# Taking unread matrix products out of the routing stage of a two-layer mixture-of-experts encoder

## The reference

```python
def expert_choice_moe(x, w_router, b_router, w_gate, w_up, w_down):
    cap = EC_CAPACITY_FACTOR * s // N_EXPERTS            # 2*512/16 = 64 tokens for each of 16 experts
    logits = (x @ w_router) + b_router                   # 512 tokens x 16 experts
    aff = jax.nn.softmax(logits, axis=-1)
    gates, idx = lax.top_k(aff.transpose(0, 2, 1), cap)  # each expert picks its 64 tokens
    xs = x[idx]
    hid = silu(xs @ w_gate[e]) * (xs @ w_up[e])          # 64x1024 @ 1024x1024, per expert
    o = (hid @ w_down[e]) * gates
    y = zeros.at[idx].add(o)                             # back to the tokens

for l in range(2):
    mix = concat(attention, short conv, conformer conv, windowed attention) @ w_out[l]
    x = layer_norm(alpha * x + mix)
    x = layer_norm(alpha * x + expert_choice_moe(x))
```

## Time and profile before

| | us |
|---|---|
| median of 3 runs | 1485.55 |
| profiled execution | 1484.97 |
| its span | 1483.0 |
| PE busy | 1368.4 (92%) |
| DVE busy | 495.6 (33%) |
| routing and expert stage, first layer | about 258 to 732 |
| routing and expert stage, second layer | about 989 to 1465 |

### The profile page before, as it was taken

One profiled execution on the slowest core, in us unless ns is written; L12 is line 12 of the kernel. 1 busy time (PEld: TensorE's weight loads), 2 busy tenths in 40 slices (PEclk: granted clock), 3 DMA queues, 4 the chain that ended last, 5 costly groups with the idle time before them and its releaser, 6 DMA issues.

```text
span 1483.0 us, 15565 instructions
## 1 busy us (share of the span) xinstructions
PE 1368.4 (92%) x6362; PEld 714.1 (48%) x6362; DVE 495.6 (33%) x999; ACT 292.5 (20%) x517; POOL 107.6 (7%) x90
## 2 busy tenths in 40 slices
PE   6999999999999999989789998999999999999884
PEld 5666668533343333333367565774343343343332
DVE  5774754410211111101449557451201201201205
ACT  2336540110000000000033456211000000000000
POOL 1330000000000000000133200000000000000001
PEclk9999999999999999999979999999999999999998
DMA  9300351999999999999960012539999999999994
GB/s 384 116 1 1 142 199 49 417 421 429 427 426 427 427 426 427 427 427 428 421 242 1 0 55 89 214 143 428 428 428 426 428 426 429 426 426 429 426 428 168
DMA packets 43685, 462.03 MB, mean 312 GB/s; under 512 B 7776, under 2 KB 8416, under 8 KB 14944
## 3 DMA queue, kind: packets, MB, share of 16 engines
q1 hardware_dynamic: 33120, 436.88, 69.8%
q0 software_dynamic: 3744, 13.63, 2.3%
q10 hardware_dynamic: 6752, 10.54, 2.1%
HBM read 450.55 MB, written 10.49 MB: 311 GB/s over the span
## 4 chain that ended last, share of the span: by engine, by line
PE 75%; DMA 12%; DVE 6%; issue 3%; ACT 3%; SPq 0%; ACTq 0%; DVEq 0%; POOLq 0%
PE bank L896 24%; PE bank L919 13%; PE bank L520 10%; DMA ring<-w_moe 10%; PE bank L864 8%; PE bank L775 2%; PE bank L779 2%; PE bank L778 2%; PE bank L757 2%; PE bank L478 2%; PE bank L835 1%; PE bank L664 1%; PE bank L941 1%; PE bank L748 1%; PE bank L852 1%
## 5 line engine op out<-in xcount | busy, mean ns | idle before, releaser
L896 PE MATMUL bank<-ring,work 128*64 128x512 f32 x1600 | 350.4, 593 | 16.2 <-issue 8.8
L896 PEld LDWEIGHTS bank<-ring,work 128*64 128x64 f32 x1600 | 131.0, 137 | 221.7 <-issue 195.7
L919 PE MATMUL bank<-ring,w_up 128*64 128x512 f32 x832 | 187.3, 600 | 16.2 <-ACT w_up L1787 10.9
L1474 DVE TENSOR_TENSOR work<-work,bank 128x512 f32<-128x512 f32 x32 | 22.0, 687 | 476.9 <-PE bank L896 476.1
L1493 DVE TENSOR_TENSOR X<-X,bank 128x512 f32<-128x512 f32 x112 | 77.0, 688 | 251.4 <-PE bank L864 251.4
L919 PEld LDWEIGHTS bank<-ring,w_up 128*64 128x64 f32 x832 | 65.2, 138 | 127.4 <-issue 109.9
L864 PE MATMUL bank<-work,cst 128*128 128x512 f32 x240 | 116.3, 617 | 9.8 <-ACT work L1808 9.8
L896 PE MATMUL bank<-work 128*64 128x512 f32 x448 | 99.0, 593 | 1.5 <-issue 1.5
L520 PE MATMUL bank<-x_hi,w_hi 128*128 128x512 f32 x288 | 82.6, 434 | 11.1 <-ACT x_hi L1561 6.2
L864 PEld LDWEIGHTS bank<-work,cst 128*128 128x128 f32 x240 | 38.5, 188 | 87.2 <-DVE X L1493 36.7
L1132 DVE SCALAR_TENSOR_TENSOR bank<-X,par,bank 128x512 f32<-128x512 f32 x120 | 79.9, 749 | 0.9 <-DVE ring L1106 0.9
(11 more groups left out here) (223 smaller groups left out, 1531.6 us busy)
## 6 DMA issues: line engine op xcount, KB each, us to landing
ring<-w_moe SPq DMA_DIRECT2D x154, 2048.0 KB, 27.4
work<-w_moe SPq DMA_DIRECT2D x36, 2048.0 KB, 22.7
ring<-w_in SPq DMA_DIRECT2D x18, 1024.0 KB, 19.9
ring<-w_out SPq DMA_DIRECT2D x8, 1024.0 KB, 32.0
out<-X POOLq DMA_DIRECT2D x12, 512.0 KB, 10.3
X<-out ACTq DMA_DIRECT2D x2, 2048.0 KB, 8.2
work<-ln SPq DMA_DIRECT2D x4, 1024.0 KB, 18.5
x_rows<-X ACTq DMA_DIRECT2D x8, 512.0 KB, 2.7
```

The lines of the kernel that those rows point to most:

```text
L896: ins = mm(B((kind, pair, n))[64 * e:64 * e + 64, :], xsT[:, k, 64 * e:64 * e + 64], w[:, e, n * 512:(n + 1) * 512], start=(k == 0), stop= ...
L919: ins = mm(B(("O", pair, n))[64 * e:64 * e + 64, :], hidT[:, k, 64 * e:64 * e + 64], w[:, i, e], start=(k == 0), stop=(k == KD - 1))
```

## The change

The function `unread` and its three calls are gone; no other instruction is added, removed or moved.

```diff
-                def unread(times):
-
-                    for i in range(times):
-                        mm(B(("O", 0, 1))[:, :], ident, cos_d[:], start=True, stop=True)
-
...
                 pe.sem_inc(freed, 1)
 
 
-                unread(1)
                 pe.wait_ge(tokens_in, at(lay, 16, 16))
                 pe.wait_ge(aff_ready, at(lay, 1, 1))
                 before(pe, ("affT",), lay)
...
                 ins.then_inc(fullsem(("affT",)), 1)
-                unread(8)
 
 
                 pe.wait_ge(edge_ready, at(lay, 1, 1))
...
                     .then_inc(fullsem(("rank",)), 1)
-                unread(1)
```

## The result

The changed kernel takes 1489.31 us (median of 9 runs, 1487.27 to 1490.42) against 1484.5 us (9 runs, 1482.56 to 1486.66) of the kernel before: ratio 1.0029, 95% interval 1.002 to 1.0039. It is 4.8 us or 0.29% slower, above the 0.2% under which the prediction would have called it no change. The time lies in the forecast range, in its upper third; the likeliest case had been +1.6 us and "no change". Its profiled execution took 1489.66 us, with a span of 1487.7 us.

The account below looks back on a forecast made before the run. The weight queue was taken to set each layer's end; PE 2.5 and 3.3 us late, less slack of 1.8 and 2.4, gave pauses of 0.7 and 0.9 us: 1484.97 + 1.6 = 1486.6 us, range 1484.0 to 1491.5.

Parts of the forecast that it names:

- the likeliest case: Whole kernel: a pause of up to 4.5 us in the weight queue, +1.6 us taken; chance 0.52.
- What bounds the kernel: From the logits on, the weight queue sets each layer's end; a late PE costs only if the queue runs empty.
- The hold-up of L811: Routing: the eight middle unread products hold up the edge product; removal gains 0.76 us in the first layer, nothing in the second.
- The chain at half clock: L811 to L823 in the routing: eleven small records at 0.12 us more each, 1.3 us per layer, between 0 and 1.4.
- The dense run after it: The gather from L835 starts at half clock for 4.0 us and loses 2.0 us per layer, between 1.4 and 2.65.
- rival B: The gather does not bring the clock back; all its records run cold, pauses together 9.2 us, 1494.2 us; chance 0.12.
- PE's lateness: After the routing PE is later than now by 2.5 us in the first layer and 3.3 us in the second.
- The first and last product cost nothing and gain nothing: The unread products before L803 and before the gather lie in waits for DVE; removing them gains nothing.
- The queue's pause: Weight queue at piece 12: PE's lateness less slack, 0.7 us in the first layer and 0.9 us in the second.
- a slack of 1.8 and 2.4 us: Queue slack at piece 12 by layer, taken 0.7 above lower ends of 1.1 and 1.7; upper ends 3.9 and 4.5.
- Rival C: PE's lateness goes through undiminished: piece 12's slack is unreal or PE sets the end; 5.8 us, 1490.8 us; chance 0.16.
- The rule that charges the whole low stretch: Penalty of half the throttled time: 14 us more low clock, 7 us lost per layer, 14 in all, 1499 us; not taken.

Follow-up runs that it names:

- late_pair3: Kernel before with four more unread products at the start of the fourth pair of experts, where the weight queue is deep; ratio 0.9996.
- slots_late: Kernel before with all products in place, but the slots of pieces 10, 11 and 12 given back one chunk of products later; ratio 1.0017.
- eight_only: Kernel before without the first and the last unread product of each layer, the eight in the middle kept; ratio 1.001.
- eight_gone: Kernel before without the eight middle unread products of each layer, the first and the last kept; ratio 1.0019.
- gone_layer0: Kernel before with the ten unread products taken out in the first layer alone; ratio 1.0003.
- gone_layer1: Kernel before with the ten unread products taken out in the second layer alone; ratio 1.0021.
- after_fetch_late: Changed kernel with the gather's last quarter put off from chunk 4 to chunk 6, freeing piece 12's slot 2.0 us earlier; ratio 1.0034 to the kernel before.
- mid_four: Kernel before with four in place of eight unread products in the middle, the first and the last kept; ratio 1.0005.
- mid_seven: Kernel before with seven in place of eight unread products in the middle, the first and last kept; ratio 0.9988, measured again 0.9986.

## Why the prediction was right, and where it was too small

- **What bounds the kernel: right.** PE's lateness is free in late_pair3, and in slots_late the late slots cost though PE is in time.
- **The hold-up of L811: half of it.** 0.76 us had been credited; L1412's end to L1417 takes 0.86 us where L1420's end to L1425 took 1.20, a gain of 0.34. The edge product starts 0.05 us after the reduction now, and the first layer still takes 0.86 us where the second takes 0.51: about half of the difference between the layers, from which the 0.76 had been read, was no hold-up.
- **The chain at half clock: right.** 4.47 us from L1417 to the gather in the first layer, 3.41 before: 1.1 us, forecast 1.3.
- **The dense run after it: right.** The gather costs 1.9 and 2.5 us more, forecast 2.0 each. The clock rises while the gather runs, so rival B has fallen: at 284 and 1017.8, forecast 284 and 1014.
- **PE's lateness: right in the first layer, short in the second.** Piece 10 is issued 2.6 us late in the first layer (forecast 2.5), and 1022.9 - 1017.7 - 0.9 = 4.3 us in the second (forecast 3.3); there the products of the logits already ran at half clock in part (L748 2.80 us, 2.18 before), which made PE 0.6 us late.
- **The first and last product cost nothing and gain nothing: wrong in part for the last one.** Without it the clock fell at the gather in one layer of two (eight_only), and with it the low stretch ends 3 to 7 us sooner (eight_gone).
- **The queue's pause, the term that was mis-sized.** Forecast 0.7 and 0.9 us, measured 3.6 and 3.8. With a slack of 1.8 and 2.4 us I had let a late piece 12 land 7.0 us behind its issue. No row shows a landing that fast; even the empty queue takes 7.6 to 7.7. A piece lands at the later of 4.9 us behind the one ahead and at least 7.6 us behind its issue. With that, piece 12 of the kernel before (302.3 for piece 11, + 4.9 = 307.2; 298.7 + 7.7 = 306.4) has 0.8 us of slack, under the 1.1 that I had called the least. In the first layer piece 12 then took 9.8 us and not 7.0, which is nearly the whole miss there. In the second it took 7.9, so 0.9 us of the miss; 1.0 us is PE's greater lateness; and 1.0 us came at piece 13, which I had not looked at and which landed 5.9 us behind piece 12. Pieces 10 to 13 are all thin, since PE gives back three of these slots 5.6 and 6.0 us apart and a piece takes 4.9. Why a late piece takes 9.8 us one time and 7.7 the next is not shown: in the first layer of gone_layer0, on PE the same instructions, piece 12 took 7.9 us and the stage was 2.7 us longer, not 3.6.
- **Missing from the sum:** the 2.75 us that come back between the layers. 1.6 had been forecast for 3.6 + 3.8 - 2.75 = 4.7. Two terms were wrong in opposite directions, and that the range held is luck: with 3.6 + 3.8 us and nothing given back the sum would have been 1492.4 us, outside it. Rival C's 5.8 us was nearer in number. Of its two reasons one has fallen: PE does not set the end, it still waits 2.8 and 2.6 us for pieces near the end of the first layer, as before. The other, that the slack at piece 12 is not real, was nearly right: the stages lost 3.6 and 3.8 us for a lateness of 2.6 and 4.3.
- **The rule that charges the whole low stretch** (the Trainium skill, page "TensorE: Matmul & The Clock Gate", section "Terms") gave an estimate of +14 us by the forecast stretches. The clock was low for 14 and 17 us longer, and the price was 4.8, so this case does not bear the rule out for a stretch that is mostly a wait.

## What to carry to other kernels

A product that nobody reads can earn its place: ask what clock the first dense run behind a wait finds, and fill the wait up to the start of that run, without holding up what comes first (seven in the middle, with 0.4 to 0.6 us of idle time left in the first layer, beat eight). When a transfer queue sets the end of a stage, PE's lateness costs nothing where the queue is deep, and where it is thin all of it that is beyond the slack; the thin place is right behind the prefetch, where the first slots are given back. Slack there is at most issue-to-landing of each piece, less that of an issue into the empty queue; it has to be reckoned for every piece until the slots come faster than the pieces, and the stage loses by the worst of them.

## What the runs showed of the hardware that was not expected

- A piece of 2048 KB takes 4.9 us in a full queue and 7.6 to 7.7 us from issue to landing in one that has long been empty; behind late slots, in a queue that has just run dry, 7.6 to 10.0 us (slots_late and gone_layer1, second layer, 7.6; after_fetch_late, piece 11, 10.0).
- Now and then a piece deep in the queue lands some 1.5 us late: 6.4 us behind the one ahead after 14.8 us in the queue (after_fetch_late, piece 20 of the second layer), at places that change from one execution to the next.
- Idle for 3.1 us after four products (mid_four), PE's clock was still up at the edge product and fell at 276.7, during the small chain behind it; with seven (mid_seven) and an idle time of 0.6 us it stayed up.
- In the first layer of eight_only the clock fell 0.7 us behind a gap of 1.7 us between the rank chain and the gather; in its second layer it stayed up over a gap of 1.5 us, and so it did in the kernel before, where one product splits the gap.
